# Eleven instead of eight seven-product pairs in each of three FFNs, with the low parts of the plain pairs' weights made by adding transfers

## The chip, the cores and the metric

The kernel runs on one core of a Trainium2 chip, as one program. The metric is device microseconds of one execution. The engines in play are TensorE (PE, matmuls; PEld are its weight loads), VectorE (DVE), ScalarE (ACT), GpSimd (POOL) and SyncE (SP, which issues the loads of weights).

## The reference

The network takes x of 512 tokens by 1024 channels through two blocks. The first block has two layers; each is an FFN, a mixer (gated linear attention in layer 0, differential attention in layer 1) and another FFN. The second block is one hybrid layer. All is float32. The change touches the FFNs alone:

```python
def swiglu_ffn(h, w_gu, w_down):
    gate, up = jnp.split(h @ w_gu, 2, axis=-1)
    return (jax.nn.silu(gate) * up) @ w_down

for i in range(DEPTH):           # DEPTH = 2: four FFNs
    x = x + 0.5 * swiglu_ffn(rms_norm(x, norm_g[i, 0]), ffn_w_gu[i, 0], ffn_w_down[i, 0])
    ...                          # a mixer
    x = x + 0.5 * swiglu_ffn(rms_norm(x, norm_g[i, 2]), ffn_w_gu[i, 1], ffn_w_down[i, 1])
```

D_FF is 2816, that is 22 tiles of 128 channels.

## The kernel before

**Splitting in three products.** Activations lie transposed, 128 channels on the partitions and 512 tokens along a row. Every float32 operand is split in a high part rounded to the matmul's type (whi, xh, ah) and a low part, the rest (wlo, xl, al). A product of a 128x128 weight tile is three matmuls: high by high, high by low, low by high (`rows`, L1836).

**Units and slots.** Weights come from HBM as panels of 1024 rows by 256 columns (1024 KB) into four raw buffers, issued by SP (`load`, L683), which loads panel n when the low part of the last unit of panel n - 4 is made. Each half of a panel (128 columns) is a unit of 8 tiles. A unit u uses weight slot u % 4. ScalarE makes its high part (`w_hi`, L720, a copy with rounding) when unit u - 4 has been used up by TensorE; VectorE then makes its low part (`w_lo`, L1213: raw minus high). Both run ahead by at most four units, and each engine works in program order, so the place of a call `w_hi(u)` or `w_lo(u)` between its other instructions sets the time; `w_lo(u)` makes the units up to u + 3.

**Pairs.** An FFN goes over 22 pairs: pair j is the gate tile and the up tile of 128 channels. A plain pair is two units and 2 x 8 x 3 = 48 matmuls of 512 columns. ScalarE's silu, VectorE's product, ScalarE's rounding into ah and VectorE's `low_part` (L1263) follow. Pairs whose numbers stand in FAST are seven-product pairs: both the tokens (two halves of 256) and the weights (gate and up, halves of the inner dimension) are treated as a 2x2 block matrix, and the four blocks come out of seven half-size products of sums, Strassen's scheme in Winograd's form. Such a pair has four units, fa, fc, fd (4 tiles) and fb, used in this order, and 7 x 4 x 3 = 84 matmuls of 256 columns (`fast_pair`, L1941). VectorE makes the sums of weights from the raw panels (`weight_sums`, L1233, four instructions, just before the low part of fa) and joins the products (`join_halves`, L1355): the first join, then the low parts that `w_lo(u + 2)` and `w_lo(u + 3)` ask for, then five more instructions. The next seven-product pair on TensorE waits for the first join of the one before it.

**Parts.** Three of the four FFNs work in parts of 8, 8 and 6 pairs; after each part come eight down projections, each of 8 (6) tiles by three matmuls. They read the activation tiles in order. The fourth FFN has no seven-product pairs.

**Order of an engine in a pair j.** VectorE: w_lo(u), w_lo(u + 1), low_part(j - 1), then the multiplications or joins of pair j, then the product of gate and up. ScalarE: w_hi(u), w_hi(u + 1); for a seven-product pair a copy of the first product out of PSUM, w_hi(u + 2), w_hi(u + 3); then silu and the rounding into ah. GpSimd sums squares for the norms at the end of a stage and issues a few transfers.

Of the kernel before, what the change touches and what calls it, by code (L numbers as in the profile page):

```python
# [6 lines left out]
F32 = mybir.dt.float32  # L7
# [11 lines left out]
NRAW = 4  # L19
# [3 lines left out]
FAST = (tuple(range(6, 22, 2)),) * 3 + ((),)  # L23
# [37 lines left out]
class Weights:  # L61


    def __init__(self):
        self.panels, self.units, self.fast = [], [], {}
# [335 lines left out]
def build(nc, a):  # L401
    with ExitStack() as ctx:
# [276 lines left out]
        def sync_program(e):  # L679
# [20 lines left out]
        def act_program(e):  # L700
# [19 lines left out]
            def w_hi(n_used_now):  # L720
                while made[0] < min(n_used_now + NSLOT, NU):
# [487 lines left out]
        def dve_program(e):  # L1209
# [3 lines left out]
            def w_lo(n_used_now):  # L1213
                while made[0] < min(n_used_now + NSLOT, NU):
# [18 lines left out]
            def weight_sums(u):  # L1233
# [8 lines left out]
                lo_done(w, u - 1)  # L1242
# [13 lines left out]
            def ffn(f):  # L1256
# [4 lines left out]
                for part, (k0, n) in enumerate(parts):  # L1261
# [8 lines left out]
                    for j in range(k0, k0 + n):  # L1270
# [31 lines left out]
                        if f == 1 and j == 6:  # L1302
                            w.wait_ge(sem["bias_vec"], 16)
# [84 lines left out]
            def ada_pair(n):  # L1388
# [161 lines left out]
            def diff():  # L1550
                u = first["diff"]
                zero_halves(dparts)
                for s in DS:
# [40 lines left out]
                    elif s[0] == "attend":  # L1594
# [72 lines left out]
            def hybrid():  # L1667
# [20 lines left out]
                for s in HS:  # L1688
# [59 lines left out]
                    elif s[0] == "attend":  # L1748
# [4 lines left out]
                        w.wait_ge(sem["h_in"], 32)  # L1753
# [71 lines left out]
        def pe_program(e):  # L1825
# [60 lines left out]
            def ffn(f):  # L1886
# [6 lines left out]
                for part, (k0, n) in enumerate(FF_PARTS[f]):  # L1893
                    for j in range(k0, k0 + n):
# [26 lines left out]
                        if f == 1 and j == 2:  # L1921
                            w.wait_ge(sem["onehot"], 16)
# [350 lines left out]
            def hybrid():  # L2273
# [7 lines left out]
                for s in HS:  # L2281
# [116 lines left out]
        def pool_program(e):  # L2398
# [18 lines left out]

            def out_squares(n):
# [11 lines left out]
            def position_bias():  # L2430
                w.wait_ge(sem["x_lo"], 24)
                e.dma_start(onehot[:, :], a["onehot"]).then_inc(sem["onehot"], 16)
                w.wait_ge(sem["bias_rows"], 2)
                e.dma_start(bias_vec, bias_rows[:, :]).then_inc(sem["bias_vec"], 16)
                w.wait_ge(sem["bias_vec"], 16)
                e.dma_start(bias_rep.rearrange("h (r c) -> h r c", c=1024),
                            bias_vec.unsqueeze(1).broadcast_to([8, 128, 1024])).then_inc(sem["bias_rep"], 16)

            def load_bias(h):
                src = bias_rep[h, 127:127 + 128 * 1023].rearrange("(p c) -> p c", c=1023)[:, 0:896]  # L2440
                w.wait_ge(sem["bias_rep"], 16)
# [3 lines left out]
                e.dma_start(bt[h % 2][:, :], src).then_inc(sem[f"d_bias{h % 2}"], 16)  # L2445
# [8 lines left out]
            def load_ada(n):  # L2454
# [136 lines left out]
```

## Time and profile before

| | us |
|---|---|
| median of 3 runs | 2210.42 (2210.36 to 2210.47) |
| profiled execution | 2210.79 |
| its span | 2209.0 |

The span is 1.8 us shorter than the execution's time. The profile counts an engine as busy while an instruction of it runs. Matmuls are pipelined, and the starts of consecutive matmuls are nearer than their durations; so the spacing of starts is what a matmul costs. On VectorE too an instruction starts some 0.1 us before the one ahead has ended. The granted TensorE clock of this run is 1.0. The three FFNs with seven-product pairs are the stretches from about 13 to 375 us, from about 625 to 985 us and from there to about 1340 us.

### The profile page before, as it was taken

The numbers are of one execution on the slowest core, as the hardware profiler recorded it, in microseconds if no ns is written. First come the engines' busy times: TensorE is split into PE (matmuls) and PEld (weight loads), VectorE is DVE, ScalarE is ACT, GpSimd is POOL, SyncE is SP. The second block draws the span as 40 slices with busy tenths as digits, with TensorE's granted clock in tenths as the row PEclk, the third lists the DMA queues.
The fourth block names the chain that finished last, engine by engine and source line by source line (L and its number), as shares of the span: only waits on it lengthen the run. The fifth ranks groups of instructions, "written<-read, shape, count | busy, mean of one in ns | idle before, by whom it ended". The sixth has DMA issues, their size and how long they took to land.

```text
span 2209.0 us, 27070 instructions
## 1 busy us (share of the span) xinstructions
PE 2194.8 (99%) x10808; PEld 1800.3 (81%) x10808; DVE 1450.7 (66%) x2245; ACT 989.3 (45%) x1542; POOL 155.0 (7%) x127
## 2 busy tenths in 40 slices
PE   9999999999999999999999999999999999999999
PEld 7889897877778898988898887777788888877777
DVE  6757476988757574766566677777576536555863
ACT  5424234567544242334333336777442222238672
POOL 3000003000030000030000011000210000020000
PEclk9999999999999999999999999999999999999999
DMA  6323234131125223332324232222144334242211
GB/s 195 115 77 115 77 105 129 39 96 58 58 79 191 96 85 107 96 115 77 115 77 134 76 103 87 83 74 85 58 153 143 124 115 134 91 134 77 76 59 39
DMA packets 201597, 217.67 MB, mean 99 GB/s; under 512 B 4776, under 2 KB 194344, under 8 KB 201472
## 3 DMA queue, kind: packets, MB, share of 16 engines
q1 hardware_dynamic: 194768, 193.48, 27.1%
q0 software_dynamic: 6560, 22.39, 3.0%
q8 instruction: 86, 1.41, 0.3%
q14 instruction: 39, 0.32, 0.1%
q10 hardware_dynamic: 144, 0.08, 0.0%
HBM read 213.79 MB, written 6.32 MB: 100 GB/s over the span
## 4 chain that ended last, share of the span: by engine, by line
PE 93%; DVE 3%; ACT 3%; issue 1%; DMA 0%; POOL 0%; SPq 0%; DVEq 0%; ACTq 0%
PE ps L1829 92%; PE ps L1833 1%; DVE sb_wlo L1230 1%; ACT sb_whi L715 1%; DMA sb_xT<-xT 0%; ACT sb_xh L715 0%; DVE sb_xT L1334 0%; ACT sb_hyb_th L715 0%; DVE sb_xl L1252 0%; ACT sb_lnb L715 0%; ACT L706 0%; DVE sb_gla_eq L1538 0%; DVE sb_gla_ek L1535 0%; ACT sb_hyb_pt L715 0%; ACT sb_hyb_k L715 0%
## 5 line engine op out<-in xcount | busy, mean ns | idle before, releaser
L1829 PE MATMUL ps<-sb_xh,sb_whi 128*128 128x512 f32 (+1 forms) x2016 | 770.3, 382 | 1.8 <-DVE sb_xl L1618 0.8
L1829 PE MATMUL ps<-sb_xl,sb_whi 128*128 128x512 f32 (+1 forms) x2016 | 753.0, 375 | 0.1
L1829 PE MATMUL ps<-sb_xh,sb_wlo 128*128 128x512 f32 (+1 forms) x2016 | 750.9, 375 | 0.0
L715 ACT ACTIVATE sb_whi<-sb_raw 128x1024 fp32r<-128x1024 f32 (+1 forms) x376 | 378.3, 1016 | 410.6 <-PE ps L1829 403.3
L1230 DVE TENSOR_TENSOR sb_wlo<-sb_raw,sb_whi 128x1024 fp32r<-128x1024 f32 (+1 forms) x328 | 408.7, 1252 | 207.2 <-ACT sb_whi L715 203.6
L1829 PEld LDWEIGHTS ps<-sb_xh,sb_whi 128*128 128x128 f32 x2016 | 379.9, 188 | 85.0 <-issue 18.1
L1829 PEld LDWEIGHTS ps<-sb_xl,sb_whi 128*128 128x128 f32 x2016 | 380.1, 189 | 69.4 <-issue 3.3
L1829 PEld LDWEIGHTS ps<-sb_xh,sb_wlo 128*128 128x128 f32 x2016 | 379.6, 188 | 69.6
L1829 PE MATMUL ps<-sb_ffn_ah,sb_whi 128*128 128x512 f32 x704 | 274.3, 390 | 0.0
L1829 PE MATMUL ps<-sb_ffn_ah,sb_wlo 128*128 128x512 f32 x704 | 273.9, 389 | 0.0
L1829 PE MATMUL ps<-sb_ffn_al,sb_whi 128*128 128x512 f32 x704 | 273.9, 389 | 0.0
L1829 PEld LDWEIGHTS ps<-sb_ffn_ah,sb_wlo 128*128 128x128 f32 x704 | 132.2, 188 | 27.7
L1829 PEld LDWEIGHTS ps<-sb_ffn_al,sb_whi 128*128 128x128 f32 x704 | 132.2, 188 | 27.3
L1829 PEld LDWEIGHTS ps<-sb_ffn_ah,sb_whi 128*128 128x128 f32 x704 | 132.2, 188 | 27.2
L1334 DVE SCALAR_TENSOR_TENSOR sb_xT<-ps,sb_xT 128x512 f32<-128x512 f32 x88 | 60.5, 687 | 132.3 <-PE ps L1829 132.2
L715 ACT ACTIVATE sb_ffn_vgw<-sb_ffn_vgw 128x512 f32<-128x512 f32 x66 | 41.8, 633 | 227.9 <-DVE sb_ffn_vgw L1377 127.1
L715 ACT ACTIVATE sb_ffn_ah<-sb_ffn_u 128x512 fp32r<-128x512 f32 x88 | 55.6, 632 | 143.1 <-DVE sb_ffn_u L1308 124.8
L1829 PE MATMUL ps<-sb_ffn_th,sb_whi 128*128 128x256 f32 x384 | 108.7, 283 | 0.0
L1829 PE MATMUL ps<-sb_ffn_tl,sb_whi 128*128 128x256 f32 x384 | 108.7, 283 | 0.0
L1829 PE MATMUL ps<-sb_ffn_th,sb_wlo 128*128 128x256 f32 x384 | 108.7, 283 | 0.0
L2404 POOL TENSOR_TENSOR sb_sqs<-sb_xT 128x512 f32<-128x512 f32 x7 | 9.2, 1314 | 1241.9 <-DVE sb_xT L1334 928.3
L1296 DVE TENSOR_TENSOR sb_ffn_u<-ps,sb_rb 128x512 f32<-128x512 f32 x64 | 44.0, 688 | 60.2 <-PE ps L1829 60.2
(295 smaller groups left out, 2563.4 us busy)
## 6 DMA issues: line engine op xcount, KB each, us to landing
sb_raw<-ffn_w_gu SPq DMA_DIRECT2D x86, 1024.0 KB, 5.1
sb_raw<-ffn_w_down SPq DMA_DIRECT2D x32, 1024.0 KB, 5.3
sb_raw<-gla_w_in SPq DMA_DIRECT2D x12, 1024.0 KB, 5.4
sb_raw<-diff_w_in SPq DMA_DIRECT2D x12, 1024.0 KB, 5.1
sb_ada_raw<-w_ada POOLq DMA_DIRECT2D x12, 1024.0 KB, 6.1
sb_raw<-w_in SPq DMA_DIRECT2D x10, 1024.0 KB, 5.2
sb_raw<-ffn_w_down SPq DMA_DIRECT2D x12, 768.0 KB, 4.6
sb_raw<-gla_w_out SPq DMA_DIRECT2D x4, 1024.0 KB, 5.3
```

Source lines behind the costliest of these rows:

```text
L715: return e.activation(out, in_, func, bias=bias, scale=scale)
L1230: e.tensor_tensor(lo, raw[panel % NRAW][:, 0:nk, off:off + 128], hi.bitcast(F32), ALU.subtract).then_inc(sem["w_lo"], 1)
L1296: e.tensor_tensor(v, psum[banks[1]][:, :], rb[:, :], ALU.mult).then_inc(sem["f_u"], 1)
L1334: e.scalar_tensor_tensor(out=x[:, m, :], in0=psum[f_banks[f]["down", (part, m)][0]][:, :], scalar=0.5, in1=x[:, m, :], op0=ALU.mult, op1=A ...
L1829: return e.matmul(out, lhsT, rhs, start=start, stop=stop, skip_group_check=skip)
L1833: ins = e.transpose(psum[bank][:, c * 128:(c + 1) * 128], src[:, c * 128:(c + 1) * 128], ident)
L2404: e.tensor_tensor(sqs[:, :], x[:, 0, :], x[:, 0, :], ALU.mult).then_inc(sem["sq"], 1)
```

## The change

FAST becomes pairs 6, 7, 9, 10, 12, 13, 15, 16, 18, 19 and 21, where it was 6, 8, ..., 20. The units of the plain pairs above 6 (8, 11, 14, 17 and 20) are listed in `by_dma`, ten an FFN. For those ScalarE first writes the negated weights into the slot's low part (rounded by the same write), then the high part as before; VectorE leaves them out; GpSimd waits for the negation and issues a transfer from the raw panel onto wlo, with addition. raw plus the negated rounded weight is the low part. `lo_done`, by which TensorE and SP wait, waits for the transfer's semaphore of the slot in such a unit. To free semaphores for it, several small ones are merged (bias, ada and hybrid inputs). Core of the diff:

```diff
-FAST = (tuple(range(6, 22, 2)),) * 3 + ((),)
+FAST = ((6, 7, 9, 10, 12, 13, 15, 16, 18, 19, 21),) * 3 + ((),)
...
+                    if fast and k0 + 2 * j + half > 6:
+                        self.by_dma += [len(self.units), len(self.units) + 1]
                     self.unit(gate, 128 * half, "gate")
                     self.unit(up, 128 * half, "up")
...
+        vector_low, dma_low = [], {}
+        for u in range(NU):
+            if u in W.by_dma:
+                dma_low[u] = 16 * (1 + sum(v % NSLOT == u % NSLOT for v in dma_low))
+            vector_low.append(u + 1 - len(dma_low))
+
         def lo_done(w, u):
-            w.wait_ge(sem["w_lo"], u + 1)
+            if u in dma_low:
+                w.wait_ge(sem["w_hi"], u + 1)
+                w.wait_ge(sem[f"low{u % NSLOT}"], dma_low[u])
+            else:
+                w.wait_ge(sem["w_lo"], vector_low[u])
...
-                    lo_done(w, W.panels[n - NRAW][3])
+                    for u in range(W.panels[n - NRAW][3] + 1):
+                        if W.units[u][0] == n - NRAW or u == W.panels[n - NRAW][3]:
+                            lo_done(w, u)
...
-                        act(whi[u % NSLOT][:, 0:nk, :], raw[panel % NRAW][:, 0:nk, off:off + 128],
-                            ACT.Copy).then_inc(sem["w_hi"], 1)
+                        src = raw[panel % NRAW][:, 0:nk, off:off + 128]
+                        if u in dma_low:
+
+                            act(wlo[u % NSLOT][:, 0:nk, :], src, ACT.Copy, scale=-1.0).then_inc(sem["w_neg"], 1)
+                        act(whi[u % NSLOT][:, 0:nk, :], src, ACT.Copy).then_inc(sem["w_hi"], 1)
...
+                    if u in dma_low:
+                        continue
...
-                lo_done(w, u - 1)
+                w.wait_ge(sem["w_lo"], vector_low[u - 1])
...
+            def low_parts(f):
+
+                for n, u in enumerate(W.by_dma):
+                    if ffn_of(u) == f:
+                        panel, off, nk, _ = W.units[u]
+                        w.wait_ge(sem["w_neg"], n + 1)
+                        e.dma_start(wlo[u % NSLOT][:, 0:nk, :].bitcast(F32), raw[panel % NRAW][:, 0:nk, off:off + 128],
+                                    accum_op=ALU.add).then_inc(sem[f"low{u % NSLOT}"], 16)
...
+            low_parts(0)
             ffn_squares(0, KT)
             gla()
             out_squares(0)
             position_bias()
+            low_parts(1)
             ffn_squares(1, KT)
+            low_parts(2)
             ffn_squares(2, KT)
```

## Rows read from the trace of the kernel before

**Rows 1.** Page, part 1: busy time, share of the span, instructions.
```profile
PE 2194.8 (99%) x10808; PEld 1800.3 (81%) x10808; DVE 1450.7 (66%) x2245; ACT 989.3 (45%) x1542; POOL 155.0 (7%) x127
```

**Rows 2.** Chain of waits, 90 to 400 us: start, length, what.
```profile
89.87 285.30 PE ps L1829 x1548
```

**Rows 3.** Windows over pair 10 (seven products) and pair 11 (plain) of FFN 0.
```profile
core 0: us, PE busy (x) PEld busy (x) DVE busy (x) ACT busy (x) POOL busy (x), PEclk, DMA share, GB/s
162.82:172.90 10.08, 10.08 (x86) 10.08 (x85) 7.82 (x10) 5.21 (x7) 0.00 (x0) 1.00 0.33 106
172.90:183.80 10.90, 10.90 (x51) 9.00 (x49) 8.71 (x13) 3.07 (x5) 0.00 (x0) 1.00 0.29 96
```

**Rows 4.** Timeline of PE around the start and end of pair 10: start, length.
```profile
162.82 0.28 PE L1829 MATMUL ps<-sb_xh,sb_whi 128*128 128x256 f32 x1
...
172.65 0.28 PE L1829 MATMUL ps<-sb_ffn_tl,sb_whi 128*128 128x256 f32 x1
172.77 0.28 PE L1829 MATMUL ps<-sb_ffn_th,sb_wlo 128*128 128x256 f32 x1
172.89 0.40 PE L1829 MATMUL ps<-sb_xh,sb_whi 128*128 128x512 f32 x1
173.12 0.40 PE L1829 MATMUL ps<-sb_xl,sb_whi 128*128 128x512 f32 x1
```

**Rows 5.** Timeline of DVE from pair 10 into pair 11.
```profile
166.15 1.23 DVE L1223 TENSOR_TENSOR sb_wlo<-sb_raw,sb_whi 128x1024 fp32r<-128x1024 f32 x1 [1.65 <-ACT sb_whi L715]
167.29 1.22 DVE L1230 TENSOR_TENSOR sb_wlo<-sb_raw,sb_whi 128x1024 fp32r<-128x1024 f32 x1
168.43 0.68 DVE L1267 TENSOR_TENSOR sb_ffn_al<-sb_ffn_u,sb_ffn_ah 128x512 fp32r<-128x512 f32 x1
169.03 0.68 DVE L1363 TENSOR_TENSOR sb_ffn_vgw<-sb_ffn_sums,ps 128x512 f32<-128x512 f32 x1
169.86 1.23 DVE L1230 TENSOR_TENSOR sb_wlo<-sb_raw,sb_whi 128x1024 fp32r<-128x1024 f32 x1 [0.15 <-ACT sb_whi L715]
171.22 0.69 DVE L1243 TENSOR_TENSOR sb_ffn_sums<-sb_raw 128x512 f32<-128x512 f32 x1
...
173.89 1.22 DVE L1223 TENSOR_TENSOR sb_wlo<-sb_raw,sb_whi 128x1024 fp32r<-128x1024 f32 x1
175.02 0.68 DVE L1369 TENSOR_TENSOR sb_ffn_vgw<-sb_ffn_vgw,ps 128x512 f32<-128x512 f32 x1
...
178.06 0.69 DVE L1305 SCALAR_TENSOR_TENSOR sb_ffn_u<-sb_ffn_u,sb_ffn_vgw 128x512 f32<-128x512 f32 x1
```

**Rows 6.** Timeline of ACT in pairs 10 and 11.
```profile
165.08 1.99 ACT L715 ACTIVATE sb_whi<-sb_raw 128x1024 fp32r<-128x1024 f32 x2
...
178.79 0.63 ACT L715 ACTIVATE sb_ffn_ah<-sb_ffn_u 128x512 fp32r<-128x512 f32 x1 [0.77 <-DVE sb_ffn_u L1305]
179.33 1.04 ACT L715 ACTIVATE sb_whi<-sb_ffn_sums 128x1024 fp32r<-128x1024 f32 x1
```

**Rows 7.** Page, part 5: high and low parts of plain units, whole span.
```profile
L715 ACT ACTIVATE sb_whi<-sb_raw 128x1024 fp32r<-128x1024 f32 (+1 forms) x376 | 378.3, 1016 | 410.6 <-PE ps L1829 403.3
L1230 DVE TENSOR_TENSOR sb_wlo<-sb_raw,sb_whi 128x1024 fp32r<-128x1024 f32 (+1 forms) x328 | 408.7, 1252 | 207.2 <-ACT sb_whi L715 203.6
```

**Rows 8.** DMA view: queue, count, KB each, median us to landing.
```profile
sb_raw<-ffn_w_gu SPq DMA_DIRECT2D x86, 1024.0 KB, 5.1
sb_ada_raw<-w_ada POOLq DMA_DIRECT2D x12, 1024.0 KB, 6.1
bias_rep<-bias_vec POOLq DMA_DIRECT2D x1, 4096.0 KB, 26.7
sb_dif_bias<-bias_rep POOLq DMA_DIRECT2D x8, 448.0 KB, 3.5
sb_raw<-ffn_w_gu SPq DMA_DIRECT2D x4, 512.0 KB, 9.3
sb_gla_mask<-mask POOLq DMA_DIRECT2D x1, 512.0 KB, 3.8
```

**Rows 9.** Timeline of DVE behind pair 7, the last plain pair of part 1.
```profile
98.52 0.69 DVE L1296 TENSOR_TENSOR sb_ffn_u<-ps,sb_rb 128x512 f32<-128x512 f32 x1 [1.39 <-PE ps L1829]
99.31 0.69 DVE L1308 TENSOR_TENSOR sb_ffn_u<-sb_ffn_u,sb_ffn_vgw 128x512 f32<-128x512 f32 x1
100.70 0.69 DVE L1267 TENSOR_TENSOR sb_ffn_al<-sb_ffn_u,sb_ffn_ah 128x512 fp32r<-128x512 f32 x1 [0.70 <-ACT sb_ffn_ah L715]
```

More of the change, by code:

```diff
@@ L64, in __init__ @@
     def __init__(self):
-        self.panels, self.units, self.fast = [], [], {}
+        self.panels, self.units, self.fast, self.by_dma = [], [], {}, []
     def panel(self, w, k0, nk, c0, nc):
@@ L384 @@
 par cst xin0 xin1 xin2 xin3 raw0 raw1 raw2 raw3 w_hi w_lo w_used out_k
+w_neg low0 low1 low2 low3
 x_hi x_lo sq sq_first sq_add sq_last norm lnb warm
@@ L387 @@
 s_add t_act t_vec f_join
-zero onehot bias_mm bias_rows bias_vec bias_rep
-ada0 ada1 ada_col ada_mm ada_add silu_c sp_act sp
+zero bias_dma bias_mm bias_rows
+side0 side1 ada_col ada_mm ada_add silu_c sp_act sp
 g_in g_lr g_q g_k g_v g_vT g_vrow g_g g_silu g_zmm g_nb g_rbT g_zact g_z g_x0
 g_dk g_dq g_exp g_mk g_c g_x g_t g_mq g_level g_at g_atc g_o g_osq g_oss g_on g_y g_yhi g_ylo
-d_bias0 d_bias1 d_lam d_lam_mm d_lam_e d_neg d_qb_q d_qb_k d_sq_q d_sq_k d_ss d_qk_q d_qk_k
+d_lam d_lam_mm d_lam_e d_neg d_qb_q d_qb_k d_sq_q d_sq_k d_ss d_qk_q d_qk_k
 d_hi_q d_hi_k d_lo_q d_lo_k d_v d_vT d_vrow
 d_score d_max d_exp d_comb d_turn d_pt d_pv d_osq d_oss d_y d_yhi d_ylo
-h_in gs h_z h_hi h_conv0 h_conv h_gmm h_gates h_r h_i h_ix h_tanh h_a h_ln h_m h_sqrt h_one h_b h_scan
+gs h_z h_hi h_conv0 h_conv h_gmm h_gates h_r h_i h_ix h_tanh h_a h_ln h_m h_sqrt h_one h_b h_scan
 h_sq h_ss h_qk h_part h_other h_v h_vT h_vrow h_score h_max h_exp h_comb h_turn h_pt h_pv h_ya
@@ L1302, in ffn @@
                         if f == 1 and j == 6:
-                            w.wait_ge(sem["bias_vec"], 16)
+                            w.wait_ge(sem["bias_dma"], 32)
                         if fast:
@@ L1752, in hybrid @@
                         w.wait_ge(sem["h_score"], n + 1)
-                        w.wait_ge(sem["h_in"], 32)
+                        w.wait_ge(sem["g_in"], 64)
                         if n >= 3:
@@ L1921, in ffn @@
                         if f == 1 and j == 2:
-                            w.wait_ge(sem["onehot"], 16)
+                            w.wait_ge(sem["bias_dma"], 16)
                             w.wait_ge(sem["lnb"], ln_done(("norm", 2)))
@@ L2304, in hybrid @@
                         i = s[1]
-                        w.wait_ge(sem["h_in"], 32)
+                        w.wait_ge(sem["g_in"], 64)
                         w.wait_ge(sem["h_conv"], 3 * i + 3)
@@ L2431, in position_bias @@
                 w.wait_ge(sem["x_lo"], 24)
-                e.dma_start(onehot[:, :], a["onehot"]).then_inc(sem["onehot"], 16)
+                e.dma_start(onehot[:, :], a["onehot"]).then_inc(sem["bias_dma"], 16)
                 w.wait_ge(sem["bias_rows"], 2)
-                e.dma_start(bias_vec, bias_rows[:, :]).then_inc(sem["bias_vec"], 16)
-                w.wait_ge(sem["bias_vec"], 16)
+                e.dma_start(bias_vec, bias_rows[:, :]).then_inc(sem["bias_dma"], 16)
+                w.wait_ge(sem["bias_dma"], 32)
                 e.dma_start(bias_rep.rearrange("h (r c) -> h r c", c=1024),
-                            bias_vec.unsqueeze(1).broadcast_to([8, 128, 1024])).then_inc(sem["bias_rep"], 16)
+                            bias_vec.unsqueeze(1).broadcast_to([8, 128, 1024])).then_inc(sem["bias_dma"], 16)
             def load_bias(h):
                 src = bias_rep[h, 127:127 + 128 * 1023].rearrange("(p c) -> p c", c=1023)[:, 0:896]
-                w.wait_ge(sem["bias_rep"], 16)
+                w.wait_ge(sem["bias_dma"], 48)
                 w.wait_ge(sem["x_lo"], 40)
@@ L2458, in load_ada @@
                     w.wait_ge(sem["ada_col"], KT * (n - 1))
-                e.dma_start(ada_raw[n % 2][:, :, :], src).then_inc(sem[f"ada{n % 2}"], 16)
+                e.dma_start(ada_raw[n % 2][:, :, :], src).then_inc(sem[f"side{n % 2}"], 16)
             def hybrid():
                 w.wait_ge(sem["f_x"], last_x(3, KT - 1))
-                e.dma_start(causal[:, :], a["causal"]).then_inc(sem["h_in"], 16)
-                e.dma_start(lw, a["lru_w"]).then_inc(sem["h_in"], 16)
+                e.dma_start(causal[:, :], a["causal"]).then_inc(sem["g_in"], 16)
+                e.dma_start(lw, a["lru_w"]).then_inc(sem["g_in"], 16)
             e.dma_start(cst[:, :, :], a["cst"]).then_inc(sem["cst"], 16)
```

6 lines of the change are left out of this document (3 added, 3 removed).

## The prediction

> **What bounds the kernel now.** I read the busy table first: TensorE is busy for 2194.8 of 2209.0 us and the next engine, VectorE, for 1450.7 [rows 1]. The chain of waits inside the first FFN then says that this busyness is the path: from 89.87 us on it is one unbroken run of 1548 matmuls, 285.30 us long, with no other engine in it [rows 2]. So in the FFNs every column that TensorE is spared is a gain, and every wait put in front of it is a loss, one for one.
>
> The windows over one seven-product pair and the plain pair behind it price both: 10.08 us and 10.90 us, TensorE busy throughout, granted clock 1.00 in both [rows 3]. That agrees with the starts of matmuls: 84 of 256 columns, 0.12 us apart, against 48 of 512 columns, 0.2266 us apart [rows 4]. Below, F is a seven-product pair and P a plain one. VectorE has 7.82 us busy in the F window and 8.71 in the P window [rows 3]: it does work of an F while TensorE is already in the P that follows. Before the change each F has such a P behind it.
>
> **The gain.** Each FFN goes from 8 to 11 F. 9 pairs in three FFNs, each 10.90 - 10.08 = 0.82 us shorter: -7.4 us [rows 3]. Nothing else on TensorE changes.
>
> **What VectorE and ScalarE must do in an F.** I take T as the start of F10 at 162.82 [rows 4] and shift the rows behind it. When another F follows instead of a P, VectorE's order, read from the code, is: low part of the pair's last unit fb (T+3.33), then the four sums of the next pair, 1.36 us after that start in the same order of work (169.86 to 171.22), so T+4.69; low part of the next fa 2.67 later, T+7.36; 1.13 later low_part of the activation, T+8.49; the first join T+9.09 (done T+9.8, and TensorE's next F, which waits for it, starts at T+10.08: in time by 0.3); low parts of the next fc T+9.69 and fd T+10.83; the second join T+11.45 [rows 5]. In the row of before that join sits at 175.02, and 3.04 us later the product of gate and up (178.06), 0.73 later ScalarE's copy into ah (178.79), 0.54 later the high part of the next pair's fb (179.33) [rows 5, 6]. Shifted: T+14.49, T+15.22, T+15.76. The high part takes 1.06, so the low part of fb starts at about T+16.85 and ends 1.22 later, T+18.1 with the hop. TensorE wants it after 60 of 84 products of the second F: T+10.08+7.20 = T+17.28.
>
> (a) **A stall of 0.8 us in the second F of every two.** These are pairs 7, 10, 13 and 19: 4 an FFN, 3.2 us. The bounds: 0.3 (if 0.5 us of the shifts are generous) and 1.3.
>
> **The transfers.** Ten units an FFN (pairs 8, 11, 14, 17, 20) lose VectorE's subtraction, 30 x 1252 ns off VectorE, and ScalarE gets as many negations at 1016 ns [rows 7]. ScalarE is at 45%, VectorE at 66% [rows 1], so neither sum matters; the order does. For a P behind two F, ScalarE cannot reach the negation before it has copied ah of the first F and made the high part of fb: T+15.76, two such copies take 1.99 in a row [rows 6], so the negation ends at T+17.75 and GpSimd can issue at about T+17.8. TensorE is through the second F at T+20.16, with (a) at T+20.96, and then waits for the whole low part before its first matmul. That leaves the transfer **3.2 us**. The second unit of such a P is negated 2.1 us later and wanted 5.45 us later, so it is never the later one.
>
> What the transfer takes, call it D, no row shows: nothing in the trace adds onto memory or goes from SBUF to SBUF. From below: GpSimd's transfers of 448 KB land in 3.5 us and its one of 512 KB in 3.8. From above: four 512 KB transfers landed in 9.3. Between them: 1024 KB land in 5.1 when SP issues them and 6.1 when GpSimd does [rows 8]. An adding transfer of 512 KB has to read 1024 KB (the source and the target), so I take the row that is GpSimd's and moves 1024 KB, 6.1 us. That is an estimate from that row.
>
> (b) **A stall of D - 3.2 = 2.9 us in each P behind two F.** Pairs 11, 14 and 20: 3 an FFN, 8.7 us. At 3.8 it is 1.8 an FFN, at 9.3 it is 18.3. For P17, which has only one F in front of it, the same count gives: fa16 is used up at 2.9, negation 3.0 to 4.0, wanted at 10.08, room 6.0; so 0.1 at D = 6.1 and 3.3 at 9.3. P8 has its slots freed during the eight down projections (5.44 us each) and costs nothing. GpSimd has no other work there, its squares come behind the last down projection of an FFN.
>
> (c) **F as the last pair ahead of the down projections.** Down projections read the activation tiles in order, the last tile after 7 x 3 matmuls (4.76 us), or 5 x 3 (3.40 us) in the third part. Before, the last pair was a P: from the end of its matmuls at 98.5 to the start of the last low part 100.70 and its end 101.4 are 2.9 us, in time [rows 9]. Behind an F there are 3.04 + 0.73 + 0.63 of the same rows plus 0.68 for the low part and the hops: done 5.35 us after its end. That gives 0.6 at pair 15 and 2.0 at pair 21. Pair 7 is moreover the second of two F; VectorE's queue is then low part fb (T+16.85), two low parts of down units with low_part and the first join between them, and one more low part, so the second join starts at T+22.6 and the last activation tile is ready at T+27.7, against 20.96 + 4.76 = 25.7 wanted: 2.0. Together 4.6 an FFN; bounds 3 and 6.
>
> **Edits at nothing.** The merged semaphores wait for counts that are reached as before. SP's reload of a panel now waits for a transfer instead of a subtraction; the panels of pairs 10 and 11 are wanted again for pair 14, some 25 us on, and two panels land in about 10 us [rows 8]: covered. Should D be near 10, that cover still holds. Contention between the transfers and the panel loads: both at once take longer, but the loads behind P11 are released by its own transfer, so they are not beside it. The position bias copy of 4096 KB precedes FFN 1's transfers in GpSimd's queue; it is issued in FFN 1's fourth pair and lands in 26.7 us, before pair 8.
>
> **The sum.** An FFN: 3.2 + 8.8 + 4.6 - 2.5 = 14.1 us, three of them 42.4. The profiled execution took 2210.8 (span 2209.0), 0.4 above the median; so 2253.2 and, in the median's terms, **2253 us**.
>
> The page "DMA: Bandwidth & Descriptors" of the Trainium skill gives, in the section "Anatomy of one DMA — SWDGE (gpsimd) path", a fit of about 2.0 us plus bytes over 436e3: 3.2 us for these 512 KB. The rows bear it out only roughly, 3.8 where the fit says 3.2. By it (b) would vanish, and the sum would be 2210.4 + 3 x (3.2 + 4.6 - 2.5) = 2226; its case is rival 1, priced there from a row.
>
> **The rivals.**
> 1. *The addition costs the transfer nothing*: it lands as a load of its size, 3.8 us [rows 8]. For it: the payload is only 512 KB. Against it: two streams have to be read. (b) falls to 1.8, an FFN costs 7.1 net, 2232 us.
> 2. *The addition is slow*: D near 9.3, as the slowest 512 KB row. For it: rows of 512 bytes on GpSimd's queue, for which no row speaks. (b) 21.6 with P17, an FFN 26.9 net, 2291 us.
> 3. *Faster*: the lookahead of four weight slots does absorb the second F, and the transfers land in time. Its place is the low part of fb and the negation of the P behind; its price is the shorter columns alone, -7.4 us, 2203 us. It decides once D is under 3.2 and the queue of two F is 0.8 us shorter than I shift it. For it: from start to start, VectorE needs for an F 2.67 (sums), 3 x 1.14 + 0.6 (low parts), 0.6 (first join), 3.04 + 0.6 (the rest up to the product) and 0.6 (low_part), 11.5 us, and for a P without low parts 2.6 [rows 5]; over F F P that is 25.6 of TensorE's 31.1 us. Against it: every start in [rows 5, 6] is bound by order, not by load.
> 4. *Half of it*: (a) and (b) hold about zero, (c) about what is gained. Within 0.2%, 2210.
>
> **How the numbers follow.** Forecast 0.54, rival 1 0.16, rival 2 0.17 (0.06 of it beyond 2292), rival 3 0.09, rival 4 0.04. Some 0.2% (4.4 us) is what a measurement of this kernel can tell from no change. Faster 0.09, same 0.04, slower 0.87. The range goes from 2218 to 2292: with (a) and (c) at their low bounds and the transfer as in rival 1 an FFN costs 1.2 + 1.8 + 3.0 - 2.5 = 3.5 us net, 2221 us, and 3 us below it are for what rivals 3 and 4 share with it; the upper end is rival 2. Outside it lie 0.13 below and about 0.06 above.
>
> **What would show it.** TensorE's waits list gets rows that are absent now: on low parts in the FFNs (the transfers' tile wlo, 9 times, 2 to 4 us each, and 12 times below 1 us on VectorE's subtraction of the seven-product units), and on sb_ffn_al ahead of the down projections, 9 times. The DMA view shows 30 adding transfers, landing in about 6 us. VectorE's group of sb_wlo from sb_raw shrinks by 30 and the join rows grow from 24 to 33. I am wrong if TensorE's chain stays unbroken through pairs 9 to 11, if the transfers land under 3.2 us, or if the second join of an F behind an F starts less than 0.5 us after TensorE has left it.

## The result, and the profile after

The changed kernel takes 2324.77 us (median of 4 runs, 2322.89 to 2326.33) against 2210.44 us (4 runs, 2210.36 to 2211.23) of the kernel before on the same chip: a ratio of 1.0517, 95% interval [1.0502, 1.0531]. 2253 was forecast, with a range that ended at 2292: the direction was right, the size was off by 72 us, and the time lies outside the range. The profiled execution has a span of 2324.5 us, 115.5 more than before.

The busy times of the page, which answer to [rows 1]:

```profile
PE 2221.2 (96%) x11132; PEld 1827.4 (79%) x11132; DVE 1473.2 (63%) x2305; ACT 1031.7 (44%) x1599; POOL 201.6 (9%) x157
```

The shares look harmless, yet TensorE, which had been at 99%, is at 96%. Its own list of waits (what it waited for, us in total, times, longest) has six rows that the kernel before doesn't have:

```profile
PE ps L1849 <- DMA sb_wlo<-sb_raw: 56.5, 10, 8.8
PE ps L1849 <- DVE sb_ffn_al L1287: 11.8, 9, 1.8
PE ps L1849 <- DVE sb_ffn_u L1393: 8.0, 2, 4.0
PE ps L1849 <- DVE sb_wlo L1243: 7.1, 12, 0.6
PE ps L1849 <- DVE sb_ffn_vgw L1383: 3.4, 3, 1.4
PE ps L1849 <- DVE sb_xT L1354: 2.5, 1, 2.5
```

The third row is misnamed. A wait for several semaphores is put down to the one that came last, and here a join on VectorE and a transfer end together; TensorE's code waits for the transfer, not for that join. The wait is in pair 11, whose transfer was issued at 175.13 us and landed 7.1 later, at 182.2; TensorE started at 182.32. So the transfers' waits are twelve, not ten.

The DMA view of those transfers in the changed kernel's FFN 0, one row for each of the stretches 175 to 176, 214 to 215, 297 to 298 and 333 to 334 us (the gate units of pairs 11, 14, 17 and 20; the last number is us to landing):

```profile
sb_wlo<-sb_raw POOLq DMA_DIRECT2D x1, 512.0 KB, 7.1
sb_wlo<-sb_raw POOLq DMA_DIRECT2D x1, 512.0 KB, 11.9
sb_wlo<-sb_raw POOLq DMA_DIRECT2D x1, 512.0 KB, 6.8
sb_wlo<-sb_raw POOLq DMA_DIRECT2D x1, 512.0 KB, 10.8
```

Two of them land in about 7 us and two in about 11 and 12. SyncE's timeline, beside GpSimd's, shows what lies beside the slow ones: two panel loads are issued 0.11 us behind the transfer of pair 14.

```profile
214.03 1.53 POOL L2444 DMA_DIRECT2D sb_wlo<-sb_raw  x1 [35.22 <-ACT sb_wlo L730]
216.20 1.52 POOL L2444 DMA_DIRECT2D sb_wlo<-sb_raw  x1 [0.63 <-ACT sb_wlo L730]
```
```profile
214.14 1.00 SPq L702 DMA_DIRECT2D sb_raw<-ffn_w_down  x2
```

Then the chain of waits around pair 14. It has an engine's work, the negation, the transfer, and TensorE:

```profile
212.70 1.05 ACT sb_wlo L730
213.75 0.28 issue
214.03 11.86 DMA sb_wlo<-sb_raw
225.89 0.14 issue
226.03 4.06 PE ps L1849 x10
```

And the windows over this stall. The column before the last two is TensorE's granted clock, 1.00 for 2.4 GHz and 0.50 for 1.2:

```profile
217.00:219.00 2.00, 0.24 (x3) 0.04 (x1) 1.97 (x4) 0.80 (x1) 0.72 (x1) 1.00 1.02 320
219.00:222.00 3.00, 0.00 (x0) 0.00 (x0) 2.96 (x6) 0.18 (x1) 0.00 (x0) 1.00 1.14 263
222.00:224.00 2.00, 0.00 (x0) 0.00 (x0) 1.08 (x2) 1.23 (x3) 0.00 (x0) 0.62 1.24 245
224.00:226.00 2.00, 0.00 (x0) 0.00 (x1) 1.17 (x1) 0.79 (x1) 0.00 (x0) 0.50 1.43 189
226.00:228.00 2.00, 1.97 (x5) 1.61 (x6) 0.05 (x1) 0.00 (x0) 0.00 (x0) 0.50 1.45 183
228.00:230.00 2.00, 2.00 (x8) 1.57 (x7) 0.00 (x0) 0.00 (x0) 0.00 (x0) 0.68 0.14 21
230.00:232.00 2.00, 2.00 (x11) 1.62 (x10) 0.00 (x0) 0.00 (x0) 0.00 (x0) 1.00 0.00 0
```

TensorE's last matmul of pair 13 ends at 217.25 us. The granted clock falls to 0.50 while the engine is idle, and pair 14 then begins at half clock. The timeline of its matmuls shows the price: starts 0.43 us apart in place of 0.2266 [rows 4].

```profile
226.03 0.77 PE L1849 MATMUL ps<-sb_xh,sb_whi 128*128 128x512 f32 x1 [8.78 <-DMA sb_wlo<-sb_raw]
226.59 0.63 PE L1849 MATMUL ps<-sb_xl,sb_whi 128*128 128x512 f32 x1
227.02 0.63 PE L1849 MATMUL ps<-sb_xh,sb_wlo 128*128 128x512 f32 x1
```

**The account.** I went through the starts of TensorE's matmuls over the whole span. For a matmul with a wait I count its distance from the one before less the regular spacing (0.2266 us, or 0.12 for 256 columns); for one without a wait whose distance is 1.3 to 2.6 times the regular one, the excess goes into a row of its own. Not all of that row is clock: the kernel before has 69.3 us of it at a clock of 1.00 throughout, for matmuls of the other stages stand further apart. Of the changed kernel's 96.2 us, 24.2 lie in stretches of granted clock 0.50.

| us | changed kernel, against before |
|---|---|
| waits for transfers (12) | 66.4 |
| last activation tile ahead of the down projections (9) | 13.3 |
| low part of fb in the second F (12) | 9.0 |
| first join, start of pair 7 (3) | 3.9 |
| bank of x, start of FFN 2 (1) | 2.7 |
| wide spacing without a wait, mostly half clock (96.2 against 69.3 before) | 26.9 |
| nine shorter pairs | -7.4 |
| sum (measured: 115.5) | 114.8 |

It closes to within 1 us. What follows asks whether the named causes are causes.

### The profile page after: what moved, and what is told of

Same layout as the page of the kernel before. It is cut to its first block, busy times and chain, and to the rows that moved or that the text cites. A ratio compares the mean times of both kernels' runs of the same rounds, so it can differ in the third digit from the quotient of the medians.

```text
span 2324.5 us, 28081 instructions
## 1 busy us (share of the span) xinstructions
PE 2221.2 (96%) x11132; PEld 1827.4 (79%) x11132; DVE 1473.2 (63%) x2305; ACT 1031.7 (44%) x1599; POOL 201.6 (9%) x157
## 3 DMA queue, kind: packets, MB, share of 16 engines
q0 software_dynamic: 37760, 38.12, 8.8%
## 4 chain that ended last, share of the span: by engine, by line
PE 72%; DVE 14%; ACT 6%; DMA 4%; issue 3%; POOL 0%; DVEq 0%; SPq 0%; ACTq 0%
PE ps L1849 71%; DMA sb_wlo<-sb_raw 4%; DVE sb_wlo L1250 2%; DVE sb_wlo L1243 2%; ACT sb_whi L730 2%; PE ps L1853 1%; DVE sb_ffn_al L1287 1%; ACT sb_ffn_vgw L730 1%; DVE sb_ffn_u L1328 1%; ACT sb_ffn_ah L730 1%; DVE sb_ffn_vgw L1389 1%; DVE sb_ffn_u L1325 1%; ACT sb_ffn_th L730 1%; DVE sb_ffn_u L1393 1%; DVE sb_ffn_tl L1331 0%
## 5 line engine op out<-in xcount | busy, mean ns | idle before, releaser
L1849 PE MATMUL ps<-sb_xh,sb_whi 128*128 128x512 f32 (+1 forms) x1980 | 755.5, 382 | 72.2 <-DMA sb_wlo<-sb_raw 56.5
L1849 PE MATMUL ps<-sb_xl,sb_whi 128*128 128x512 f32 (+1 forms) x1980 | 736.1, 373 | 0.1
L1849 PE MATMUL ps<-sb_xh,sb_wlo 128*128 128x512 f32 (+1 forms) x1980 | 733.1, 373 | 0.0
L1250 DVE TENSOR_TENSOR sb_wlo<-sb_raw,sb_whi 128x1024 fp32r<-128x1024 f32 (+3 forms) x280 | 350.1, 1256 | 182.2 <-ACT sb_whi L730 179.8
L1849 PE MATMUL ps<-sb_ffn_th,sb_whi 128*128 128x256 f32 x528 | 150.6, 285 | 7.1 <-DVE sb_wlo L1243 7.1
L1849 PE MATMUL ps<-sb_ffn_tl,sb_whi 128*128 128x256 f32 x528 | 149.4, 283 | 0.0
L1849 PE MATMUL ps<-sb_ffn_th,sb_wlo 128*128 128x256 f32 x528 | 149.4, 283 | 0.0
L1243 DVE TENSOR_TENSOR sb_wlo<-sb_ffn_sums,sb_whi 128x1024 fp32r<-128x1024 f32 x66 | 61.8, 956 | 100.3 <-ACT sb_whi L730 100.3
L2444 POOL DMA_DIRECT2D sb_wlo<-sb_raw x30 | 46.2, 1540 | 853.2 <-ACT sb_wlo L730 853.2
```

Of the source, the lines that this page charges most:

```text
L1243: e.tensor_tensor(lo, fast_source(u), hi.bitcast(F32), ALU.subtract).then_inc(sem["w_lo"], 1)
L1250: e.tensor_tensor(lo, raw[panel % NRAW][:, 0:nk, off:off + 128], hi.bitcast(F32), ALU.subtract).then_inc(sem["w_lo"], 1)
L1849: return e.matmul(out, lhsT, rhs, start=start, stop=stop, skip_group_check=skip)
L2444: e.dma_start(wlo[u % NSLOT][:, 0:nk, :].bitcast(F32), raw[panel % NRAW][:, 0:nk, off:off + 128], accum_op=ALU.add).then_inc(sem[f"low{u % ...
```

## The experiments

Theory A: the transfers' latency, stretched by panel loads beside it, and the half clock that their stalls bring are the loss. Theory B: two F in a row overload VectorE, whatever makes the low parts. Each experiment has the time of the kernel before beside it, on its own chip, and its ratio is to that.

### 1. Low parts on VectorE again, eleven F kept

```diff
-                    if fast and k0 + 2 * j + half > 6:
+                    if False:
```

> The eleven seven-product pairs of the changed kernel stay, but every low part is VectorE's again: no negations, no adding transfers. Theory A (the transfers and the half clock behind their stalls are the loss): of the idle time of TensorE in FFN 0 of the changed kernel only the waits on VectorE remain, 0.7 us in each second F (2.8), 1.5 at the start of pair 7 and 4.4 ahead of the down projections, 8.7 us, less 2.5 for the shorter columns: +6.2 us an FFN, 2229 us. Theory B (two F in a row overload VectorE, the transfers only come on top): VectorE gets ten more low parts an FFN, 12.5 us of work, and the stalls behind two F stay: 2270 us or more.

Measured 2245.94 us, ratio 1.0160 [1.0145, 1.0175]. The transfers cost the changed kernel 79 us. But 2245.9 is 17 above A's number; the waits list says where:

```profile
PE ps L1849 <- DVE sb_ffn_al L1287: 13.0, 9, 1.8
PE ps L1849 <- DVE sb_wlo L1243: 7.5, 12, 0.6
PE ps L1849 <- DVE sb_ffn_vgw L1383: 7.3, 6, 1.4
PE ps L1849 <- DVE sb_xT L1354: 2.8, 1, 2.8
```

The first two were counted. The first join is late six times, ahead of pairs 7 and 13, where the changed kernel showed three. Pair 13 may be new because VectorE has the low parts of P11 to make; no run shows that alone. The wait on x at the start of FFN 2 was left out of the number, and so was the clock. By the same account these waits are 35.1 us between starts and the wide spacing 7.3; with -7.4 for the shorter pairs that is 35.0, where the span grew by 34.3. So A holds for most of the loss. The rest, 35 us, is there without any transfer; whether it is VectorE's load, as B has it, or something else is asked by experiments 6 to 8.

### 2. Transfers, but no two F in a row

```diff
-FAST = ((6, 7, 9, 10, 12, 13, 15, 16, 18, 19, 21),) * 3 + ((),)
+FAST = (tuple(range(6, 22, 2)),) * 3 + ((),)
```

> The eight seven-product pairs of the kernel before (6, 8, ..., 20), with the adding transfers for the low parts of the eight plain pairs 7, 9, ..., 21 of an FFN. Theory A: a plain pair behind one F leaves a transfer 6.0 us from its issue, as pair 17 of the changed kernel, where it took 6.8 and TensorE waited 1.3 us; eight such pairs an FFN, 10 us, 24 of them 31 us: 2241 us, and the granted clock stays at 1.00 because no stall is longer than 2 us. Theory B (it is the two F in a row): no change or a small gain from VectorE's relief, 2208 to 2212 us.

Measured 2258.83 us, ratio 1.0218 [1.0201, 1.0235]: 18 us slower than A said, and B's number for this kernel is out. The kernel of before plus the transfers alone is 48 us slower.

```profile
PE ps L1849 <- DMA sb_wlo<-sb_raw: 32.5, 22, 5.8
PE ps L1849 <- DVE sb_ffn_vgw L1397: 3.4, 1, 3.4
```

A's number for a stall, 1.3 us, was that of pair 17. It held for most: of the 24 stalls, 20 are 1.1 to 1.6 us between starts. What A had not counted is pair 7, behind the first F, with 3.5, 5.9 and 3.4 us in the three FFNs, one of 2.9 (pair 15 of FFN 0), and the clock: 7.7 us more of wide spacing than before, 6.1 of it at a granted clock of 0.50.

### 3. The same transfer without the addition

```diff
-                        e.dma_start(wlo[u % NSLOT][:, 0:nk, :].bitcast(F32), raw[panel % NRAW][:, 0:nk, off:off + 128],
-                                    accum_op=ALU.add).then_inc(sem[f"low{u % NSLOT}"], 16)
+                        e.dma_start(wlo[u % NSLOT][:, 0:nk, :].bitcast(F32), raw[panel % NRAW][:, 0:nk, off:off + 128]
+                                    ).then_inc(sem[f"low{u % NSLOT}"], 16)
```

> The changed kernel, but the transfer writes the raw weights over the slot and does not add (the low parts are wrong, so the output is too). It tells what the addition costs a transfer. Theory A1 (two streams have to be read): a transfer falls from about 7 us alone and 11 to 12 beside others to 4 to 5 and 6 to 7; the stalls behind two F fall from 4.2, 8.9 and 7.9 to about 1, 3 and 3 us, and the run takes about 2255 us. Theory A2 (rows of 512 bytes between two places of SBUF, or the number of descriptors, are what is slow): the times to landing stay at 7 and 11 to 12 and the run at 2320 us.

One execution: 2283.38 us. The transfers of pairs 11 and 14 (issued at 174.24 and 207.09 us):

```profile
sb_wlo<-sb_raw POOLq DMA_DIRECT2D x1, 512.0 KB, 3.8
sb_wlo<-sb_raw POOLq DMA_DIRECT2D x1, 512.0 KB, 8.4
```

Without loads beside it the copy lands in 3.8 us, as the load of its size [rows 8], and the adding one in 7.1: the addition costs 3.3 us. Beside two panel loads of 1024 KB it is 8.4 against 11.9: the loads cost 4.6 and 4.8 us, about the same for either transfer. At pair 20, where the loads are of 768 KB, it is 7.6 against 10.8. The queue's rows of the pages (packets, MB, share of 16 engines' span), first the changed kernel, then this one:

```profile
q0 software_dynamic: 37760, 38.12, 8.8%
```
```profile
q0 software_dynamic: 10880, 38.12, 5.2%
```

Without any of these transfers the queue has 6560 packets. So an adding transfer is (37760 - 6560) / 30 = 1040 packets, a copy 144, for the same bytes. A1 and A2 each had half: the addition is the cost, but it comes as seven times the packets too, and the run can't tell the second stream from the packets. The run missed 2255 for two reasons. A1 gave the stalls beside loads 3 us, and they are 5.5 and 4.7; all stalls on transfers are 33.6 us where A1 had 21. And A1 took the half clock as gone, but 18.7 us of wide spacing over before's stay.

### 4. Panel loads kept behind the transfers

```diff
+                    for u in range(W.panels[n - NRAW][3] + 1, W.panels[n - NRAW][3] + 3):
+                        if u in dma_low:
+                            lo_done(w, u)
                 e.dma_start(raw[n % NRAW][:, 0:nk, 0:nc_], src).then_inc(sem[f"raw{n % NRAW}"], 16)
```

> The changed kernel, but SP's loads of panels that the second F of two sets free wait also for the two transfers of the plain pair behind it. Theory A with contention: in pairs 14 and 20 the first transfer took 11.9 and 10.8 us beside panel loads, in pair 11, where no load runs, 7.1. Without the loads beside them all three take about 7, the stalls of pairs 14 and 20 fall from 8.9 and 7.9 to about 4.2, 8.4 us an FFN, and the half clock behind them gets shorter: about 2324 - 25 - 3 = 2296 us. Rival: the second transfer of the same pair, 2.2 us behind, is what slows the first; then nothing changes, 2320 to 2328 us.

Measured 2297.94 us, ratio 1.0398 [1.0382, 1.0413]. TensorE's first matmul of pair 14 (its wait is misnamed as above) and SyncE's two loads, which now come behind both transfers:

```profile
220.44 0.47 PE L1852 MATMUL ps<-sb_xh,sb_whi 128*128 128x512 f32 x1 [3.98 <-DVE sb_ffn_u L1396]
```
```profile
223.85 0.99 SPq L705 DMA_DIRECT2D sb_raw<-ffn_w_down  x2
```

All three transfers behind two F in FFN 0 now land in 7.1 us, and TensorE's distance from start to start ahead of pairs 11, 14 and 20 is 4.27, 4.26 and 4.29 us, where it was 4.27, 9.06 and 8.00. The transfer of the pair's second unit runs 2.2 us behind in both kernels, so it is not what slowed the first one. 27 us for a few added waits in SyncE's queue: contention with loads was a third of the transfers' cost. It is all in the waits, which fall from 66.4 to 40.5 us. The wide spacing hardly moves, 25.5 us over before's where it was 26.9: nine waits of 4.1 us bring about as much half clock as a mixture of 4 and 9 does.

### 5. High parts first: work under the transfer

```diff
+                            elif u in dma_low:
+                                for k in range(2):
+                                    w.wait_ge(sem["w_hi"], u + k + 1)
+                                    for t in range(KT):
+                                        mm(psum[banks[k]][:, :], whi[(u + k) % NSLOT][:, t, :], XH[t], t == 0, False)
+                                        mm(psum[banks[k]][:, :], whi[(u + k) % NSLOT][:, t, :], XL[t], False, False)
+                                for k in range(2):
+                                    lo_done(w, u + k)
...
```

> The changed kernel, but in a plain pair whose low parts are transferred TensorE takes the high parts of both units first (32 matmuls, 7.25 us) and then both low parts, so real work lies under the transfer. The stalls of pairs 11, 14, 17 and 20 in FFN 0 of the changed kernel were 4.2, 8.9, 1.3 and 7.9 us. Theory A (these waits and the half clock behind them are most of the loss): about 0, 1.7, 0 and 0.7 are left, 60 us less in three FFNs, and of the 28 us of half clock some 20 go too; 2324.8 - 80 = 2245 us, near e1_vector_low, whose other stalls it keeps. Against: the gate unit's slot and bank come free 3.6 us later, which may open a new wait in the next pair; then 2260 us. Rival: the transfers slow the engines' own accesses to SBUF, and the loss stays with them wherever TensorE waits: 2300 us.

Measured 2257.60 us, ratio 1.0213 [1.0198, 1.0229].

```profile
PE ps L1849 <- DMA sb_wlo<-sb_raw: 12.2, 12, 2.2
PE ps L1849 <- DVE sb_ffn_al L1287: 11.9, 9, 1.8
PE ps L1849 <- DVE sb_wlo L1243: 7.6, 12, 0.6
PE ps L1849 <- DVE sb_ffn_vgw L1383: 5.6, 9, 1.4
```

The longest wait for a transfer falls from 8.8 to 2.2 us, all of them from 66.4 to 14.1 between starts, and the wide spacing from 26.9 us over before's to 8.6. 67 us of the loss go, with the same transfers running. The rival, that they slow the engines, is out. The time is 13 us above A's number. Half of that is in the transfers' waits, 14.1 where A left 7.2. The join row has nine waits where there were three; the six new ones are 0.5 us each. Whether they come from the later gate unit, as the expectation allowed for, or from the lost slack of the wait in front is not shown.

### 6. Two orders inside the F, low parts on VectorE

First ScalarE's high part of the next fb, ahead of silu:

```diff
                             w_hi(u + 3)
+                            w_hi(u + 4)
                             u += 2
```

> e1_vector_low (2245.9 us) with one call moved: in a seven-product pair ScalarE makes the high part of the next pair's fourth unit ahead of its silu instead of behind its copy into ah. Theory A (the stalls of 0.8 us in every second F are ScalarE's order, VectorE waiting 1.65 us there): the four stalls an FFN go and the waits for the first join (1.4 and 1.3 us an FFN) shrink as VectorE gets 1.65 us back a pair: 2245.9 - 9.6 - 4 = 2232 us. Theory B (VectorE's load over two F is the limit): the stalls move to the next wait and at most 4 us are gained, 2242 us or more.

Measured 2227.42 us, ratio 1.0078 [1.0064, 1.0092]: 18.5 us less than experiment 1, more than A said. VectorE's timeline in pair 7 shows it. With the old order (experiment 1):

```profile
93.33 0.69 DVE L1325 SCALAR_TENSOR_TENSOR sb_ffn_u<-sb_ffn_u,sb_ffn_vgw 128x512 f32<-128x512 f32 x1
95.68 1.23 DVE L1243 TENSOR_TENSOR sb_wlo<-sb_raw,sb_whi 128x1024 fp32r<-128x1024 f32 x1 [1.65 <-ACT sb_whi L730]
```

With the new one:

```profile
93.29 0.69 DVE L1326 SCALAR_TENSOR_TENSOR sb_ffn_u<-sb_ffn_u,sb_ffn_vgw 128x512 f32<-128x512 f32 x1
93.90 1.22 DVE L1244 TENSOR_TENSOR sb_wlo<-sb_raw,sb_whi 128x1024 fp32r<-128x1024 f32 x1
```

The 1.65 us in brackets, the same ones as in [rows 5], were not load but order. All twelve waits for the low part of fb are gone (9.5 us between starts), and the join is late three times, not six (4.3 us). The rest of the 18.5 us is some 2 us ahead of the down projections and 2 of wide spacing. B, in its form of load, had at most 4 us here and is out for these stalls.

Then TensorE's wait at the start of an F, for what its bank needs:

```diff
-                    w.wait_ge(sem["f_join"], 4 * i - 3)
+                    w.wait_ge(sem["t_act"], 3 * t_before[f + 1] + i)
```

> e5_hi_ahead and on top TensorE's wait at the start of a seven-product pair is for ScalarE's copy of the last first product out of PSUM (what that bank needs) instead of VectorE's first join. Theory A: the 1.6 us ahead of pair 7 and of pair 13 shrink to the wait for the low part of fa, which ends 1.2 us before that join; against e5 2 to 4 us less in three FFNs, about 2229 us. What is left ahead of the down projections (4.7 us an FFN) and at the start of FFN 2 (3 us) stays. Rival: the low part of fa is just as late, no difference.

Measured 2231.62 us, ratio 1.0096 [1.0082, 1.0109]. The join's row is gone, but nothing is gained: VectorE is as late, and in pair 7 the gap ahead of the down projections grows from 1.86 to 2.70 us between starts. After the longer one the windows show the clock at 0.50 for 106 to 108 us, after the shorter one 1.00. A wait taken off one place came back behind it, with some half clock.

### 7. F moved off the ends of the parts

With both orders of experiment 6, and ScalarE's early high part in plain pairs as well:

```diff
-FAST = ((6, 7, 9, 10, 12, 13, 15, 16, 18, 19, 21),) * 3 + ((),)
+FAST = ((6, 8, 9, 11, 12, 14, 16, 17, 19, 20),) * 3 + ((),)
...
                         act(gb[j % 2], gb[j % 2], ACT.Silu).then_inc(sem["f_silu"], 1)
+                        w_hi(u)
```

> e6_join_wait with the seven-product pairs moved off the ends of the parts, ten an FFN: 6, 8, 9, 11, 12, 14, 16, 17, 19, 20, and the same call of the high part ahead of ah in plain pairs too. If the stalls of e6 are those of last pairs (4.7 us an FFN) and of the start of FFN 2, and those inside are gone by the order, then nothing stalls and ten shorter pairs against eight give 2 x 0.82 x 3 = 4.9 us: 2205.7 us, faster than before. If two F in a row still cost 0.4 us or more each (12 of them), 2210 us or slower.

Measured 2205.07 us (9 runs), ratio 0.9976 [0.9966, 0.9985]: faster than before, by 5.4 us, at the number expected. The new places of the F and the early high part in plain pairs came in the same run, so what each gives is not told apart. The chain of waits through FFN 0 is what [rows 2] was:

```profile
59.81 270.24 PE ps L1851 x1587
```

> As e7_ten_inside with nine: 6, 8, 9, 11, 12, 14, 16, 18, 20. Two adjacent sets an FFN instead of four. Without stalls 3 x 0.82 = 2.5 us less than before, 2208.1 us; if adjacent F cost, less than e7.

Nine F (6, 8, 9, 11, 12, 14, 16, 18, 20): 2207.54 us, ratio 0.9987 [0.9978, 0.9996]. 8, 9 and 10 pairs stand at 2210.5, 2207.5 and 2205.1: 2.5 to 3 us for each more in three FFNs, where the columns say 2.5.

### 8. Eleven inside, and the transfers once more

```diff
-FAST = ((6, 8, 9, 11, 12, 14, 16, 17, 19, 20),) * 3 + ((),)
+FAST = ((6, 8, 9, 10, 12, 13, 14, 16, 17, 19, 20),) * 3 + ((),)
```

> e7_ten_inside (2205.1 us) with eleven seven-product pairs, three in a row twice: 6, 8, 9, 10, 12, 13, 14, 16, 17, 19, 20. VectorE keeps all low parts. Three F are 34.5 us of VectorE in 30.2 of TensorE: if the lookahead of four slots covers a deficit of 4.3 us, 2205.1 - 2.5 = 2202.6; if not, each of the six sets of three costs 1 to 3 us more than its 0.4 of gain: 2210 to 2220 us.

Measured 2206.27 us, ratio 0.9981 [0.9972, 0.9991]. Neither number: nothing stalls inside the parts, even with three F in a row, but one wait is there that ten F didn't have. So the lookahead covers three F, and B is out in its form of load for this order of work.

```profile
PE ps L1851 <- DVE sb_xT L1356: 2.5, 1, 2.5
```

Then the transfers again, with experiment 5's order in the plain pairs that have them:

> e10_eleven_inside with the adding transfers for the plain pairs 7, 11, 15, 18 and 21 and the order of e9_high_first in them. It asks whether a relief of VectorE by transfers is worth anything once their latency is covered. In pairs 15 and 21, which are last, VectorE's low_part comes after both units' use, now 3.6 us later for the gate unit. If VectorE is what stalls e10, it is 2 to 5 us faster than e10; if the transfers' latency still shows behind two or three F (10 us needed, 7.25 covered plus about 3 of lead), it is slower than e10 by some 5 us.

The run is not what the expectation says. Its edit against the changed kernel is that of experiment 7, with ten F, so six plain pairs above 6 (7, 10, 13, 15, 18 and 21) have transfers, and the DMA view counts 36 of them, not 30:

```diff
-FAST = ((6, 7, 9, 10, 12, 13, 15, 16, 18, 19, 21),) * 3 + ((),)
+FAST = ((6, 8, 9, 11, 12, 14, 16, 17, 19, 20),) * 3 + ((),)
```
```profile
sb_wlo<-sb_raw POOLq DMA_DIRECT2D x36, 512.0 KB, 9.0
```

Measured 2217.10 us, ratio 1.0031 [1.0019, 1.0043]. The same kernel without transfers is that of experiment 7, at 2205.07, not the one with eleven F: the transfers cost it 12 us. With ten F VectorE did not need the relief; with eleven it was not run, but there too VectorE stalls nothing inside the parts.

```profile
PE ps L1851 <- DMA sb_wlo<-sb_raw: 5.1, 8, 0.7
PE ps L1851 <- DVE sb_ffn_al L1289: 2.3, 3, 0.8
```

Between starts these two rows are 9.2 of the 12 us, and the wide spacing is 3.0 more than in experiment 7, none of it at a granted clock of 0.50.

### 9. The odd wait: a ring of banks

```diff
-            banks, p = {}, 0
+            banks, p = {}, int(f == 2)
```

> e10_eleven_inside (2206.3 us) with one change: the ring of six PSUM banks starts one bank further in FFN 2. With eleven seven-product pairs FFN 1 hands out 11 x 3 + 11 x 2 + 24 = 79 banks, so the first pair of FFN 2 gets the bank of FFN 1's very last down projection and waits for its sum (2.5 us in e1, e5, e10 and the changed kernel; with ten or eight pairs, 78 or 76 banks, it is one emptied earlier and there is no such wait). Theory: the wait goes, 2206.3 - 2.6 = 2203.7 us or slightly less. Rival (VectorE is late at the end of FFN 1 whatever the bank): the wait stays, 2206 us.

Measured 2202.56 us (5 runs), ratio 0.9964 [0.9951, 0.9978]: the best of all kernels here, 8.0 us under the 2210.54 of before beside it. The step from experiment 8's eleven F is 3.7 us, where the wait was 2.6 between starts. In five of that kernel's ten executions the mean granted clock was 0.999 besides, and these took some 1.7 us longer than the others; in all five here it is 1.00. The wait on x is gone from the list, and through FFN 2 TensorE's chain is one piece:

```profile
954.88 335.29 PE ps L1851 x1912
```

## Why the prediction was right or wrong

- **What failed, in the sum's own terms.** The sum had 42.4 us, the kernel lost 114.3. Term (b) was 26.4 us in three FFNs and measured 66.4, because contention with the panel loads was left out and the adding transfer alone was taken as 6.1 us. A term for the clock was not there and measured 26.9. Two waits were put at nothing: the first join at pair 7 (3.9) and the start of FFN 2 (2.7). Together these are 73.5 us; (a) and (c) came out 1.1 shorter. The kind of loss that was foretold, TensorE waiting for the transfers behind two F, was the right one.
- **The gain**, -0.82 us for each of 9 pairs: right. It enters the account as -7.4, and the versions with 9, 10 and 11 F show it in their times. Experiment 9 reaches rival 3's 2203 with it, but without the transfers and in another way than rival 3 had.
- **(a), 0.8 us in the second F of two**: right, 12 times, 9.0 us in all between starts against 9.6. In pair 7 TensorE's start of the last product pair is 0.92 us behind the one before, where 0.12 is regular. Its cause, ScalarE's high part behind ah, is shown by experiment 6.
- **"In time by 0.3" for the first join**: wrong at pair 7, where TensorE started 1.6 us late (1.72 between starts, less 0.12). I shifted pair 10's rows; behind the first six plain pairs VectorE is 1.8 us later than there: the low part of fb starts at 83.05 us in an F that began at 77.97, 5.1 us behind and not 3.33. In the kernel before this F begins at 77.34 and the same row has the same 5.1 us; it had to be read for the first F. 3.9 us in the three FFNs.

```profile
82.42 1.23 DVE L1223 TENSOR_TENSOR sb_wlo<-sb_raw,sb_whi 128x1024 fp32r<-128x1024 f32 x1 [1.65 <-ACT sb_whi L715]
```

- **(b), D - 3.2 us behind two F**: the 3.2 us held. Pair 11's stall was 7.1 - 3.0 = 4.1 us, 4.15 between starts. The size of D failed, in two steps. *Alone* I took 6.1 from GpSimd's 1024 KB row [rows 8]; it is 7.1. That is the smaller part, 1 us each. *Contention* I excluded: "the loads behind P11 are released by its own transfer, so they are not beside it". True of P11, where the last F shares its panels with the P. But in 12, 13 and 18, 19 both F share one set of panels; the low part of the second one's fb frees it, and two loads go out at 214.14, just as the transfer does at 214.03. I checked one of three cases and wrote for all. Experiment 4 shows what that was worth, 27 us.
- **Rival 2** (D at 9.3) came nearest to the time: its waits for transfers, 21.6 us an FFN, are close to the measured 22.1 (66.4 / 3). That is luck: it had one D of 9.3 everywhere, and the runs show 7.1 or less without loads beside it and 10.8 to 11.9 with them. Its time was 34 us too low, 27 of it for want of the next point.
- **The half clock** was in no term. The step that failed is the first paragraph's "every wait put in front of it is a loss, one for one". The waits of 8 to 9 us, and most of those of 4.3, cost more than themselves: 26.9 us of wide spacing in the changed kernel, and 8.6 once experiment 5 had put work under the waits.
- **(c), last pair ahead of the down projections**, 2.0, 0.6, 2.0: measured 1.9, 0.6 and 1.9 between starts in FFN 0, 13.3 in all against 13.8. Right.
- **The start of FFN 2**, 2.7 us: not seen; it is arithmetic of the code (79 banks in a ring of six), shown by experiment 9.
- **The cover of SyncE's reload and of the position bias**: held; ScalarE waits for the FFNs' weights 6.3 us in all (7.0 before).
- **The fit.** The Trainium skill's page "DMA: Bandwidth & Descriptors", in the section "Anatomy of one DMA — SWDGE (gpsimd) path", gives about 3.2 us for 512 KB. The plain copy took 3.8 here and the adding transfer 7.1, so the fit did not give the time of a transfer that adds.

The sum with the measured values in the old form would be 3 x (3.0 + 22.1 + 4.4 + 1.3 - 2.5) + 2.7 = 87.6; with 26.9 for the clock on top it is 114.5, where the span grew by 115.5.

## What to carry to other kernels

When a change turns an engine's step into a transfer, count the room from its issue to its first use in every place where it occurs, and look in each for what else the same event releases; one place stands for the others only if the same buffers are freed there. If the bounding engine must wait at all, put its independent work under the wait before tuning the wait itself, since a long wait can be paid a second time in clock: here the work under the wait gave 67 us (experiment 5), the shorter wait 27 (experiment 4). And suspect the order of instructions, not load, where an idle time of a helper recurs with the same length (here 1.65 us): moving one call gave 18.5 us.

## What the runs showed of the hardware

- A transfer within SBUF of 512 KB in rows of 512 bytes, issued by GpSimd, lands in 3.8 us if it copies and in 6.4 to 7.1 if it adds (6.4 to 6.5 mostly in pair 8, where the next one is issued 5.4 us later, 7.1 in pair 11, where it is 2.2 us later); beside two panel loads of 1024 KB in 8.4 and 11.9. GpSimd itself is held 0.88 us by the copy and 1.53 by the addition. The addition goes out as 1040 packets, the copy as 144.
- TensorE's clock after its own idle time, in FFN 0 of the changed kernel and of experiments 1 to 6, by the distance between starts: up to 2.12 us it was followed by the full clock every time, and from 4.26 to 9.06 by some microseconds of half clock every time. Between them it went either way. One of 2.55 and one of 3.63 were followed by full, one of 2.70 and one of 3.02 by half. One of 2.18 to 2.19, ahead of the last down projections, was followed by full in the changed kernel and in experiments 3 and 5, and by half in experiments 1 and 4 and both kernels of 6. What tells these apart stays open.
- In FFN 0 of the changed kernel the clock came back to full some 3 to 6 us after work began again.
